# Fused transformer kernel: the second norms computed in two halves of 256 tokens, and the activation zone moved to a multiple of 1024 bytes

## The reference, cut to what matters

```
h  = modulate(rmsnorm(x, g1), shift1, scale1)
x  = x + gate1 * (merged(h) @ w_out)            # merged: gated sum of three branches
h2 = modulate(rmsnorm(x, g2), shift2, scale2)   # the "second norm"
u  = dwconv3(h2 @ ffn_up) + b                   # 1024 -> 5632, a conv over tokens
x  = x + gate2 * ((silu(u1) * u2) @ ffn_down)   # 2816 -> 1024
```

## Time and profile before

| | us |
|---|---|
| three timed runs | 3622.59, 3631.5, 3633.3; median 3631.5 |
| profiled execution, its own time | 3623.86 |
| span of the profiled execution | 3622.0 |

### The profile page before, as it was taken

One profiled execution on the slowest core, in us unless ns is written; L12 is line 12 of the kernel. 1 busy time (PEld: TensorE's weight loads), 2 busy tenths in 40 slices (PEclk: granted clock), 3 DMA queues, 4 the chain that ended last, 5 costly groups with the idle time before them and its releaser, 6 DMA issues. The chain is left out here.

```text
span 3622.0 us, 49562 instructions
## 1 busy us (share of the span) xinstructions
PE 3462.4 (96%) x19450; PEld 2908.8 (80%) x19450; DVE 1490.3 (41%) x3012; ACT 1025.4 (28%) x2757; POOL 2029.1 (56%) x1216
## 2 busy tenths in 40 slices
PE   7999989998999999999999999999999999999999
PEld 6877677887779998889777787888899777878887
DVE  7833541234883221453455324331343555124420
ACT  2146434222202111342345312220242444112210
POOL 4465354564559998755433465665555342656655
PEclk9999999888999999999999999999999999999999
DMA  7533122321664443332111222332322111222322
GB/s 288 198 136 107 56 97 67 119 88 65 232 233 140 140 134 130 124 135 94 65 54 52 70 88 92 95 98 89 112 94 76 62 56 45 96 88 93 99 86 101
DMA packets 109881, 388.88 MB, mean 107 GB/s; under 512 B 12057, under 2 KB 16537, under 8 KB 108242
## 3 DMA queue, kind: packets, MB, share of 16 engines
q1 hardware_dynamic: 89280, 315.10, 26.0%
q10 hardware_dynamic: 20370, 70.61, 5.5%
HBM read 379.34 MB, written 6.32 MB: 106 GB/s over the span
## 5 line engine op out<-in xcount | busy, mean ns | idle before, releaser
L2602 POOL CAST whi<-raw 128x1024 fp32r<-128x1024 f32 (+1 forms) x606 | 620.9, 1025 | 1532.1 <-DMA raw<-in_w 1532.0
L2604 POOL TENSOR_TENSOR wlo<-raw,whi 128x1024 fp32r<-128x1024 f32 (+1 forms) x606 | 1422.7, 2348 | 48.5
L364 PE MATMUL ps<-hhi,whi 128*128 128x512 f32 x1704 | 675.5, 396 | 19.9 <-DVE q L1601 8.6
L366 PE MATMUL ps<-hhi,wlo 128*128 128x512 f32 x1704 | 670.5, 393 | 0.0
L365 PE MATMUL ps<-hlo,whi 128*128 128x512 f32 x1704 | 670.2, 393 | 0.0
L364 PEld LDWEIGHTS ps<-hhi,whi 128*128 128x128 f32 x1704 | 322.1, 189 | 93.1 <-DVE q L1601 9.4
L366 PEld LDWEIGHTS ps<-hhi,wlo 128*128 128x128 f32 x1704 | 321.8, 189 | 70.1
L365 PEld LDWEIGHTS ps<-hlo,whi 128*128 128x128 f32 x1704 | 322.2, 189 | 68.1
L517 PE MATMUL ps<-whi,hhi 128*128 128x256 f32 (+1 forms) x960 | 276.1, 288 | 0.0
L518 PE MATMUL ps<-wlo,hhi 128*128 128x256 f32 (+1 forms) x960 | 269.7, 281 | 0.0
L519 PE MATMUL ps<-whi,hlo 128*128 128x256 f32 (+1 forms) x960 | 269.7, 281 | 0.0
(11 more groups left out here) (419 smaller groups left out, 7013.7 us busy)
## 6 DMA issues: line engine op xcount, KB each, us to landing
raw<-in_w SPq DMA_DIRECT2D x574, 512.0 KB, 3.5
ada<-in_ada ACTq DMA_DIRECT2D x96, 512.0 KB, 4.6
raw<-in_w SPq DMA_DIRECT2D x16, 384.0 KB, 3.2
att_toe<-toe_dram ACTq DMA_DIRECT2D x12, 256.0 KB, 3.2
raw<-in_w SPq DMA_DIRECT2D x16, 192.0 KB, 2.4
x<-in_x SPq DMA_DIRECT2D x4, 512.0 KB, 9.2
cond<-in_cc ACTq DMA_DIRECT2D x2, 1024.0 KB, 7.2
kc_dram<-kc ACTq DMA_DIRECT2D x2, 1024.0 KB, 4.9
```

Of the source, the lines that this page charges most:

```text
L364: nc.tensor.matmul(o, whi[:, buf, c], hi[:, k, 0:n], start=(k == 0), stop=False)
L366: mm = nc.tensor.matmul(o, wlo[:, buf, c], hi[:, k, 0:n], start=False, stop=(k == kt - 1))
L2602: nc.gpsimd.tensor_copy(whi[:, buf, 0:c], raw[:, buf, 0:c]).then_inc(slab_hi, 1)
L2604: nc.gpsimd.tensor_tensor(wlo[:, buf, 0:c], raw[:, buf, 0:c], whi[:, buf, 0:c].bitcast(F32), ALU.subtract).then_inc(slab_split, 1)
```

## The change

It does two things. The zone's address `Z` becomes the first multiple of 1024 behind the tables, 50176. And in both layers of the second block the end of the mixer is laid out anew by `mixer_end`:

- `L["o"]` does only its first five tiles over 512 tokens. `HalfTiles` does the last three in halves: first tokens 0 to 255 of the three, then tokens 256 to 511 of the three, each a tile and a bank of its own, from slabs that stay in the ring for both.
- `L["norm2"]` becomes two norms of 256 tokens, with statistics in banks 2 and 5 and the same two work banks 3 and 4. The second applies only after the first is through (`after`).
- `Opening` opens the up projection with three tiles (`lead=3`): block k of tiles 0 and 1 over the first half as the first norm delivers it, then tile 2 over the first half (step 8), then block k of all three over the second half.
- The bank list is 0, 1, 6, 7 from there to the end of the layer.
- The accumulator of squares is the statistics bank and not the first work bank, in all norms that have one.

```diff
+ENDS = 3
-        Z = (place_at[0] - ring + 1535 - 1344) // 2048 * 2048 + 1344 + ring
-        assert Z >= place_at[0]
+        Z = (place_at[0] + 1023) // 1024 * 1024
...
+        class Opening(Part):
...
+            def tensor(self, pe, k):
+                g = self.gemm
+                if k == 0 and self.half == 0:
+                    for tile in g.tile[0:g.lead]:
+                        bank_ready(pe, tile)
+                if self.half == 0 and k == KT:
+                    for j in range(KT):
+                        self.block(pe, 2, j)
+                    return
+                pe.wait_ge(*self.norm.ready(k))
+                for t in range(2 if self.half == 0 else 3):
+                    self.block(pe, t, k)
...
+        class HalfTiles(Part):
...
+            def place(self, i):
+                if i >= 2 * self.n_out:
+                    return
+                self.slab.append(new_slab(self.row0 + self.first + i, BLOCKS) if i < self.n_out else self.slab[i - self.n_out])
+                self.tile.append(new_tile([self.slab[i]]))
...
+            def tensor(self, pe, i):
+                if i < 2 * self.n_out:
+                    a = slice(TC * (i // self.n_out), TC * (i // self.n_out) + TC)
+                    feature_tile(pe, self.tile[i], [self.slab[i]], 0, KT, self.hi[:, :, a], self.lo[:, :, a], TC)
...
-                    square = self.sq[i % 2] if i or self.acc is None else self.bufs[0]
+                    square = self.sq[i % 2] if i or self.acc is None else self.stats[0]
...
                 if k == 0:
+                    for c in self.after:
+                        dve.wait_ge(*c())
...
-            L["o"] = Gemm(f"o{l}", KT, KT, m_hi, m_lo, T, Residual(lat, 48 * l + 16), ready=L["b"].ready)
+            L["o"] = Gemm(f"o{l}", KT - ENDS, KT, m_hi, m_lo, T, Residual(lat, 48 * l + 16), ready=L["b"].ready)
+            L["o_end"] = HalfTiles(f"o{l}", KT - ENDS, ENDS, m_hi, m_lo, lat, 48 * l + 16)
...
-            L["up"] = Gemm(f"f_up{l}", 2 * FF2, KT, hhi, hlo, T, gated, ready=L["norm2"].ready)
+            L["up"] = Gemm(f"f_up{l}", 2 * FF2, KT, hhi, hlo, T, gated, lead=3)
...
+        def mixer_end(o, end, first, second, up):
...
+            opens = Opening(up, 0, first), Opening(up, 1, second)
+            place(o, 0)
+            for i in range(1, KT - ENDS):
+                place(o, i)
+                go(first, i - 1)
+                go(second, i - 1)
+            rotate([0, 1, 6, 7])
+            go(end, 0)
+            go(o, KT - ENDS)
+            go(first, 4)
+            go(second, 4)
+            go(end, 1)
+            go(first, 5)
+            go(end, 2)
+            go(first, 6)
+            go(end, 3)
+            go(first, 7, 8)
+            go(end, 4)
+            go(second, 5)
+            go(first, 9)
+            go(end, 5)
+            go(second, 6)
+            go(first, 10)
+            go(end, 6)
+            place(Ends(second, 7), 0)
+            go(first, 11)
+            go(opens[0], 0, 1)
+            place(Products(second, 7), 0)
+            go(first, 12)
+            go(second, 8)
+            go(opens[0], 2, 3, 4)
+            place(Products(second, 9), 0)
+            go(first, 13, 14, 15, 16, 17)
+            go(opens[0], 5, 6, 7, 8)
+            place(Ends(second, 9), 0)
+            go(second, *range(10, second.steps))
+            go(opens[1], *range(KT))
...
-            then_norm(L["o"], L["norm2"])
+            mixer_end(L["o"], L["o_end"], L["norm2", 0], L["norm2", 1], L["up"])
```

More of the change, by code:

```diff
@@ L393, in __init__ @@
                 self.spt = -(-kt // BLOCKS)
-                self.lead = 2 if ready is not None and kt == BLOCKS else 1
+                self.lead, self.opened = (lead if lead else 2 if ready is not None and kt == BLOCKS else 1), False
                 self.tile, self.slab = [], []
@@ L403, in place @@
                 if i < self.lead:
-                    if i == 0:
+                    if i == 0 and not self.opened:
                         for j in range(self.lead):
@@ L444, in vector, with __init__, place, block @@
                 self.epi.vector(dve, i)
+        class Opening(Part):
+            def __init__(self, gemm, half, norm):
+                self.gemm, self.half, self.norm = gemm, half, norm
+                self.steps = KT + 1 if half == 0 else KT
+            def place(self, k):
+                if k == 0 and self.half == 0:
+                    self.gemm.opened = True
+                    for j in range(self.gemm.lead):
+                        self.gemm.open(j)
+            def tensor(self, pe, k):
+                g = self.gemm
+                if k == 0 and self.half == 0:
+                    for tile in g.tile[0:g.lead]:
[7 more added lines that the diff above has]
+                    self.block(pe, t, k)
+            def block(self, pe, t, k):
+                g, a = self.gemm, slice(TC * self.half, TC * self.half + TC)
+                s, o, c = g.slab[t][0], tile_out(g.tile[t], TC, TC * self.half), slice(k * P, (k + 1) * P)
+                if self.half == 0 and k == 0:
+                    pe.wait_ge(slab_split, s + 1)
+                nc.tensor.matmul(o, whi[:, s % RING, c], g.hi[:, k, a], start=(k == 0), stop=False)
+                nc.tensor.matmul(o, whi[:, s % RING, c], g.lo[:, k, a], start=False, stop=False)
+                mm = nc.tensor.matmul(o, wlo[:, s % RING, c], g.hi[:, k, a], start=False, stop=(k == KT - 1))
+                if self.half == 1 and k == KT - 1:
+                    mm.then_inc(tile_done, 1)
@@ new lines, in program, with __init__, ready, vector @@
+        class HalfTiles(Part):
+            def __init__(self, name, first, n_out, hi, lo, s, gate):
+                self.row0, self.first, self.n_out, self.hi, self.lo, self.s, self.gate = rows[name], first, n_out, hi, lo, s, gate
+                self.steps = 2 * n_out + 1
+                self.tile, self.slab = [], []
+            def place(self, i):
[3 more added lines that the diff above has]
+                self.tile.append(new_tile([self.slab[i]]))
+            def ready(self, m, half):
+                return freed(self.tile[m - self.first + half * self.n_out])
+            def tensor(self, pe, i):
+                if i < 2 * self.n_out:
+                    a = slice(TC * (i // self.n_out), TC * (i // self.n_out) + TC)
+                    feature_tile(pe, self.tile[i], [self.slab[i]], 0, KT, self.hi[:, :, a], self.lo[:, :, a], TC)
+            def vector(self, dve, i):
+                i -= 1
+                if i < 0:
+                    return
+                m, half, t = self.first + i % self.n_out, i // self.n_out, self.tile[i]
+                o = self.s.x[:, m, TC * half:TC * half + TC]
+                dve.wait_ge(tile_done, t + 1)
+                nc.vector.scalar_tensor_tensor(o, tile_out(t, TC), mod[:, self.gate + m, self.s.c:self.s.c + 1], o,
+                                               ALU.mult, ALU.add).then_inc(tile_free[tile_bank[t]], 1)
@@ L2398, in program @@
             prior = all_free(mlp[3]) + all_free(ffn_c[3]) + [lambda: (kv_stored, 64)] + all_free(val_c1) if l == 0 else \
-                all_free(layers[0]["down"], 3)
+                all_free(layers[0]["down"], 4)
             L["angles"] = Transfers(all_free(mlp[3]) if l == 0 else all_free(layers[0]["b"], 3),
@@ L2433, in program @@
                             m_hi=m_hi, m_lo=m_lo, clear=[lambda L=L: L["att"].ready(7)] + all_free(L["c"], 3))
-            L["o"] = Gemm(f"o{l}", KT, KT, m_hi, m_lo, T, Residual(lat, 48 * l + 16), ready=L["b"].ready)
-            L["norm2"] = Norm("", [x[:, k, :] for k in range(KT)], R1024, hhi, hlo, lambda k, l=l: gg[:, l, 1, k, 0:1],
-                              lambda k, l=l: mod[:, 48 * l + 24 + k, 0:1], [pb(2, T)], [pb(3, T), pb(4, T)], lat.sq,
-                              lambda k, L=L: [L["o"].epi.ready(k)], clear=[lambda L=L: L["att"].ready(7)], acc=squares)
+            L["o"] = Gemm(f"o{l}", KT - ENDS, KT, m_hi, m_lo, T, Residual(lat, 48 * l + 16), ready=L["b"].ready)
+            L["o_end"] = HalfTiles(f"o{l}", KT - ENDS, ENDS, m_hi, m_lo, lat, 48 * l + 16)
+            for half, name in enumerate(("", "c_")):
+                a = slice(TC * half, TC * half + TC)
+                L["norm2", half] = Norm(
+                    name, [x[:, k, a] for k in range(KT)], R1024, hhi[:, :, a], hlo[:, :, a],
+                    lambda k, l=l: gg[:, l, 1, k, 0:1], lambda k, l=l: mod[:, 48 * l + 24 + k, 0:1],
+                    [pb((2, 5)[half], TC)], [pb(3, TC), pb(4, TC)], [tA[:, a], tB[:, a]],
+                    lambda k, L=L, half=half: [L["o"].epi.ready(k) if k < KT - ENDS else L["o_end"].ready(k, half)],
+                    clear=[lambda L=L: L["att"].ready(7)], acc=squares[:, a],
+                    after=[lambda L=L: L["norm2", 0].ready(7)] if half else ())
             gated = GatedConv(lat, l, 0, f_hi, f_lo, f_sums, [pb(2, T), pb(3, T)])
```

(8 more changed lines are left out.)

10 lines of the change are left out of this document (5 added, 5 removed).

## The result

The changed kernel takes **3658.0 us** (four runs, 3657.63 to 3659.09) against 3632.1 for the kernel before (four runs, 3622.59 to 3633.3): ratio 1.0077, 95% interval 1.0061 to 1.0093. It is 26 us slower. The forecast was 3621, the range 3606 to 3643: wrong in sign, and outside the range. Rival 5 (wider spacing everywhere, 3657) is what happened.

The account below looks back on a forecast made before the run. TensorE's products, busy 96% of the span, were taken to bound the kernel. The split's gain of 5.0 us a layer and 0 for the zone summed to -10, taking the median 3631.5 to 3621; range 3606 to 3643.

Parts of the forecast that it names:

- Rival 5: Zone against ring: the new relation puts 512-wide products at the wider spacing everywhere, +26 to 3657 us; chance 0.10.
- The split: Mixer end in halves: loss per layer falls from 9.92 to 4.9 us, gain 5.0 a layer, 10 in all.
- small products: Two norms of 256 tokens: their sums and spreadings now lie on TensorE's path, 1.94 us a layer.
- holes and restarts: After the projection: TensorE waits 1.2 before piece 1, 0.8 before piece 3, 0.5 later; 2.5 us a layer.
- half-wide products dearer: Projection and up tiles done in halves: products of 256 columns cost 1.4% more per column, 0.5 us a layer.
- the cover: Start of the up projection's second half: eight blocks of the third tile, 2.75 us, cover it; nothing waits again.
- the third term: Pieces after piece 3: each comes every 0.91 us for 0.69 of product; hole 0.5 with what restarts cost.
- The clock: TensorE at the openings: clock stays at its upper level; if it falls, up to 1.9 us a layer.
- The zone: Zone moved 448 bytes down, ring unmoved: taken as 0, between bounds of +36 and -10 us.
- The upper bound of that paragraph: Zone move: all products of 512 columns go to the wider spacing, +36 us.
- Rival 4: Up and down: wider spacing begins in the openings and lasts; 3635 us for both layers, 3628 for one; chance 0.10.
- The signs named beforehand: Trace after: 220 products in 50 us from 2100 to 2150 if right; 216, slow-level products or late GpSimd if wrong.

Follow-up runs that it names:

- e2: The changed kernel with the old formula for the zone (50624), so the split alone; 3616.5 us, ratio 0.9955 to the kernel before.
- e9: The same kernel as e2, timed again with more runs; 3619.2 us in 12 runs, ratio 0.9962 to the kernel before.
- e11: The split with the old zone, but an opening of two up tiles, the third done whole behind it; 3622.5 us in one run.
- e10: The split with the old zone, but all three up tiles done block by block in the first half; 3619.2 us, ratio 0.9968 to the kernel before.
- e5: The split with the zone at 50560, distance to the ring 64 bytes less than in the kernel before; 3622.4 us in one run.
- e12: The split with the zone at 50368, distance to the ring 256 bytes less than in the kernel before; 3615.5 us in one run.
- e6: The split with the zone at 50496, distance to the ring 128 bytes less than in the kernel before; 3642.2 us in one run.
- e1: The kernel before with the zone alone moved to 50176, old order of work; 3666.9 us, ratio 1.0099 to the kernel before.
- e4: The kernel before with the zone 512 bytes down, at 50112; 3642.2 us in one run.
- e3: The kernel before with the ring and small tables 448 bytes up and the zone left at 50624; 3668.9 us in one run.
- e7: The split with the zone at 50592, distance to the ring 32 bytes less than in the kernel before; 3651.3 us in one run.

## Why the prediction was wrong

**What bounds the kernel, and the loss per boundary:** right. TensorE's products set the time; less waiting and dearer products both reached the span.

**The split, forecast 5.0 a layer, measured 4.04** (70.34 - 66.30). Against the usual 0.2289, 264 whole products' worth take 60.43, so e2 loses 5.87 a layer where the forecast had 4.9:

| term | forecast | e2 |
|---|---|---|
| small products | 1.94 | 2.34 |
| holes and restarts | 2.5 | 2.56 |
| half-wide products dearer | 0.5 | 0.96 |

The sums of 256 tokens take 0.81 from their first start to the next product's (3233.62 to 3234.43) and a spreading 0.36 (3237.34 to 3237.70); there are two groups of four, 0.36 and 0.45, where the forecast had 0.50 for both together and 0.47 for a spreading. Half-wide products ran 117.8 ns apart here and not 116, which is what 1.4% over half of 228.9 gives. The 434 of the earlier trace rows could not show it: 34 of them are products of 128 columns, and in the others the weights move, while in the new ones the activations do. With the old distance both spacings, 113.4 and 117.8, occur for half-wide products of either form, and at this place of e2 and e9 the new ones had the latter. The rule of the Trainium skill on narrow products (TensorE: Matmul & The Clock Gate, Back-to-back issue gap) stays unsupported here: twice 117.8 against 228.9 is 1.03, not the 1.5 of the estimate from its figures. The places of the holes (pieces 1 and 3) and their sizes (1.2 and 0.8, measured 1.26 and 0.79 between starts) were right (a product's own 0.12 is part of the measured ones), and so was the cover (e11). Of the third term, 0.5 for later pieces and restarts, 0.1 was a hole (0.21 between starts in e2), and the seven restarts behind waits and small products took 0.65, at 0.2 to the next start instead of 0.12. GpSimd was earlier than reckoned (third slab split by T0+2.3): e10 starts the third tile 0.71 us behind the end of the projection (T0) and no wait on its weights shows.

**The clock:** half right. Before, each boundary has 6.8 us at the lower level. In e2, e9 and e10 none of six boundaries has any; in the changed kernel the second one has 3.4 us (3283.6 to 3287.0), half-wide products then being 0.21 apart, and takes 67.97 instead of 67.09. Over the ten profiled executions of a split kernel 9 of 20 boundaries have such 3.4 us. Where the other boundary of the same execution has none, they cost 0.9 (changed kernel, e5), 0.8 (e12), 0.5 (e6) and nothing (e11, 68.12 at both), less than the 1.9 that the forecast allowed.

**The zone, forecast 0, measured +34: the step that failed.** The forecast put this term of the sum at nothing, because "tiles at quite different places in the zone and in the ring run at the same spacing". They do, but all those places differ by whole multiples of 512 bytes, as the same paragraph says, and 512 is two periods of what matters: they are one and the same place, seen many times. The move by 448 was the first that left it, and the trace of before could say nothing about it. The upper bound of that paragraph, +36, then was the better number, partly by luck: it had all products of 512 columns at 233 (the real rise is 3.4 x 7,800 = 27 us) and no rise at 256 columns, where the runs show 21 us more. Some of the 48 is given back: in e1 TensorE's idle time falls by 5.9 us (159.6 to 153.7) with an unchanged order of work. That this is because what it waits for gets no slower was not tested.

**The rivals and the range.** Rival 5 named the mechanism, its sign and its price (3657, measured 3658; its -10 and +36 were -16 and +34 in e2 and e1, so part of the nearness is luck) and had a chance of 0.10 on the ground of "one spacing for nearly all places now", which is the same mistake. With an unknown between +36 and -10 and no row on it, the range should have gone to the upper bound. Rival 4 had the right observation (spacings that last after an interruption, as in e4) but not in this kernel's split: e2's up and down stand at 228.9.

**The signs named beforehand** did their work: "216 in 50 us in up and down only (4) or everywhere (5)" tells the cases apart, since 2100 to 2150, ahead of up and down, has 217 where 220 were expected.

## What to carry to other kernels

Where an operand lies relative to the other one can be worth a per cent of a kernel that is all products; treat an address change as a change to every product, and test it alone. Sameness over many places is evidence only if the places differ in what the change alters: write down their differences modulo small powers of two before saying "it makes no difference". When one edit has two parts with separate mechanisms, run them apart: here a gain of 14 to 16 us (8 of them at the two boundaries) lay hidden under a loss of 34. And look up by line what a stretch holds before its count is taken as the price of a product of your own.

## What the runs showed of the hardware

- The spacing of fp32r products at the upper clock depends on where the zone of activations lies relative to the ring of weights (e1 moved the one, e3 the other), and all eight distances fit a period of 256 bytes: 226.7, 228.9, 232.4 or 233.3 ns at 512 columns, and 113.4 to 120.0 at 256. The best place for one width is not that of the other.
- With unchanged addresses TensorE can hold either of two spacings, 228.9 or 233.3, for hundreds of microseconds (e4: first layer 233.3, second 228.9). What switches it is open. The spread of the kernel before (3617.8 to 3647.2 in 23 runs) goes with the granted clock (correlation -0.88); whether the switch has a part in it is not shown.
- A place 32 bytes off (e7) is as wide as the worst for 512 columns: 233.3 ns, x1288 in 300 us.
